# A two-layer GLA/gMLP trunk on Trainium2: in gMLP's first projection, three of five operands are made from turned ones instead of being turned

## The reference, cut to what matters

```python
for i in range(DEPTH):
    y = rms_norm(h, norm_mix[i])
    h = h + (gla_mixer if i == 0 else gmlp_mixer)(y, ...)
    h = h + swiglu(rms_norm(h, norm_ffn[i]), w_ffn_gate[i], w_ffn_up[i], w_ffn_down[i])

def gmlp_mixer(h, w_in, b_in, ln_g, ln_b, w_s, b_s, w_out):
    z = jax.nn.gelu(h @ w_in + b_in)          # w_in: 1024 x 6144
    u, v = z[..., :E], z[..., E:]             # E = 3072
    v = layer_norm(v, ln_g, ln_b)
    ...
    return (u * sv.reshape(B, S, E)) @ w_out
```

## Time and profile before

| | before |
|---|---|
| median of 3 runs | 2548.91 us (2548.80 to 2551.12) |
| the profiled execution | 2549.63 us, of which the span is 2547.8 us |
| TensorE (PE) busy | 2507.0 us, 98% of the span |
| VectorE (DVE), ScalarE (ACT), GpSimd (POOL) busy | 1742.6, 1097.1 and 1295.0 us |
| mean granted TensorE clock | 0.997 |

### The profile page before, as it was taken

One profiled execution on the slowest core, in us unless ns is written; L12 is line 12 of the kernel. 1 busy time (PEld: TensorE's weight loads), 2 busy tenths in 40 slices (PEclk: granted clock), 3 DMA queues, 4 the chain that ended last, 5 costly groups with the idle time before them and its releaser, 6 DMA issues.

```text
span 2547.8 us, 33431 instructions
## 1 busy us (share of the span) xinstructions
PE 2507.0 (98%) x11680; PEld 2079.3 (82%) x11680; DVE 1742.6 (68%) x2225; ACT 1097.1 (43%) x1943; POOL 1295.0 (51%) x984
## 2 busy tenths in 40 slices
PE   8999999999999999999999999999999999999998
PEld 6787888778888888888888888888888888888886
DVE  5255678877787765577665899865676877656556
ACT  4344555543333344454433333344544333334444
POOL 3234456645555554454666555544455555555543
PEclk9999999999999999999999999999999999999999
DMA  7674426336566558655987455687634666326864
GB/s 236 210 268 145 111 74 215 112 116 213 205 223 217 185 184 290 194 194 166 320 291 236 145 169 171 203 302 246 205 110 143 211 213 206 120 72 213 272 191 149
DMA packets 311259, 493.38 MB, mean 194 GB/s; under 512 B 32992, under 2 KB 132704, under 8 KB 311104
## 3 DMA queue, kind: packets, MB, share of 16 engines
q1 hardware_dynamic: 311104, 491.39, 58.0%
HBM read 328.24 MB, written 154.66 MB: 190 GB/s over the span
## 4 chain that ended last, share of the span: by engine, by line
PE 89%; DVE 4%; DMA 2%; issue 2%; ACT 1%; SPq 1%; POOL 0%; DVEq 0%; ACTq 0%
PE ps L657 28%; PE ps L659 28%; PE ps L658 28%; PE ps L2729 2%; DMA qk<-qk_scratch 2%; PE ps L2517 1%; PE ps L2588 1%; DVE r_all L1909 1%; DVE state L1848 0%; DVE zbuf L1821 0%; SPq L790 0%; DVE g_sb L1857 0%; DVE r_all L1884 0%; POOL w_lo_main L645 0%; DVE att L1810 0%
## 5 line engine op out<-in xcount | busy, mean ns | idle before, releaser
L733 POOL TENSOR_TENSOR ring_lo<-stg,ring_hi 128x512 fp32r<-128x512 f32 x666 | 953.7, 1434 | 897.1 <-ACT ring_hi L729 896.5
L729 ACT ACTIVATE ring_hi<-stg 128x512 fp32r<-128x512 f32 x666 | 420.6, 632 | 1060.1 <-PE ps L659 995.2
L657 PE MATMUL ps<-xh_all,ring_hi 128*128 128x512 f32 x1536 | 600.5, 391 | 1.2 <-DVE r_all L2283 0.9
L659 PE MATMUL ps<-xh_all,ring_lo 128*128 128x512 f32 x1536 | 597.8, 389 | 0.0
L658 PE MATMUL ps<-xl_all,ring_hi 128*128 128x512 f32 x1536 | 597.6, 389 | 0.0
L751 DVE TENSOR_TENSOR s_ring<-s_stage,s_ring 128x512 fp32r<-128x512 f32 x238 | 297.9, 1263 | 225.8 <-ACT s_ring L747 225.3
L657 PE MATMUL ps<-ring_hi,s_ring 128*128 128x512 f32 x1064 | 415.5, 391 | 3.1 <-DVE r_all L1909 1.6
L659 PE MATMUL ps<-ring_hi,s_ring 128*128 128x512 f32 x1064 | 414.1, 389 | 0.0
L658 PE MATMUL ps<-ring_lo,s_ring 128*128 128x512 f32 x1064 | 414.0, 389 | 0.0
L657 PEld LDWEIGHTS ps<-xh_all,ring_hi 128*128 128x128 f32 x1536 | 288.4, 188 | 61.0 <-POOL ring_lo L733 1.3
L659 PEld LDWEIGHTS ps<-xh_all,ring_lo 128*128 128x128 f32 x1536 | 288.3, 188 | 59.9
(11 more groups left out here) (262 smaller groups left out, 3642.6 us busy)
## 6 DMA issues: line engine op xcount, KB each, us to landing
s_stage<-h_scratch SPq DMA_DIRECT2D x238, 256.0 KB, 3.4
stg<-t_scratch SPq DMA_DIRECT2D x200, 256.0 KB, 3.4
h_scratch<-r_all SPq DMA_DIRECT2D x34, 1024.0 KB, 5.1
h_scratch<-r_all SPq DMA_DIRECT2D x80, 256.0 KB, 3.5
stg<-in_w_ffn_gate SPq DMA_DIRECT2D x34, 512.0 KB, 4.3
stg<-in_w_ffn_up SPq DMA_DIRECT2D x34, 512.0 KB, 5.7
stg<-in_w_ffn_down SPq DMA_DIRECT2D x66, 256.0 KB, 3.6
t_scratch<-r_all SPq DMA_DIRECT2D x28, 512.0 KB, 2.8
```

Of the source, the lines that this page charges most:

```text
L657: pe.matmul(bank, s_hi, m_hi, start=first, stop=False, skip_group_check=more)
L659: return pe.matmul(bank, s_lo, m_hi, start=False, stop=last, skip_group_check=more)
L729: nc.scalar.activation(weight_slot(ring_hi, g), weights(g), ACT.Copy).then_inc(wh_done, 1)
L733: nc.gpsimd.tensor_tensor(weight_slot(ring_lo, g), weights(g), f32(weight_slot(ring_hi, g)), ALU.subtract).then_inc(wl_done, 1)
```

## The change

- `V_TURNS` keeps eight turned tiles: S2 (r = 8 to 11) behind steps 3, 4 and 5, A22 (now r = 16 to 19) behind steps 9 and 10. S1, S4 and S3 are no longer turned.
- ScalarE now copies each turned A11, A12 and S2 tile twice, once as it is into a kept place (`v_kept`) and once into `xh`. VectorE makes the turned S1 = S2 + A11, S4 = A12 - S2 and S3 = A22 - S2 from those (`turned_sum1`, `turned_sum4`, `turned_sum3`), and `made_hi` and `made_lo` cut them, from SBUF instead of PSUM.
- `sum4` in `head` and GpSimd's `sum3` are gone for this phase. The statistics of the first quarter, `stat(k, 0, ...)`, move from j = 10 to j = 17 in all three blocks.
- Waits and counts follow: among them SP waits at i = 17 for 12 turned tiles instead of 16 and at i = 23 for all rests of x, and TensorE's first step of product 6 asks for 12 instead of 16 rests, product 5 for `sum3_done`, product 3 for 24 instead of 28.

```diff
+        a11_kept = place("a11_kept", XH_AT + 8 * TILE, [P, 4, BANK])
+
+        s2_kept = place("s2_kept", XH_AT + 24 * TILE, [P, 4, BANK])
...
-        TURNS = {"U": ("S2", "S4", "S1", "S3", "A22"), "V": ("S2", "S1", "S4", "S3", "A22")}
+        TURNS = {"U": ("S2", "S4", "S1", "S3", "A22"), "V": ("S2", "S1", "A22", "S4", "S3")}
...
-        V_TURNS = {3: (8, 9), 4: (10,), 5: (11, 12), 6: (13, 14, 15), 9: (16, 17), 10: (18, 19), 13: (20, 21, 22, 23),
-                   14: (24, 25, 26, 27)}
+
+        V_TURNS = {3: (8, 9), 4: (10,), 5: (11,), 9: (16, 17), 10: (18, 19)}
...
+        def turns_before(n):
+
+            return 28 * n - (12 if n >= 2 else 0)
+
+        def turn_count(n, kind, r):
+
+            return turns_before(n) + r + 1 - (4 if kind == "V" and r >= 16 else 0)
+
+        def sum1_count(n, k):
+            return 4 * n + (4 if n >= 2 else 0) + k
+
+        def v_kept(op, t):
+
+            return {"A11": a11_kept[:, t, :], "S1": a11_kept[:, t, :], "A12": r_all[:, 2 * t + 1, :],
+                    "S2": s2_kept[:, t, :], "S3": n_all[:, t, :], "S4": r_all[:, 8 + 2 * t, :]}[op]
...
-                    sp.wait_ge(op_turned, 28 + 8 + 8)
-                    sp.wait_ge(sum4_done, 8)
+                    sp.wait_ge(op_turned, turns_before(1) + 8 + 4)
+                if i == 23:
+                    sp.wait_ge(xl_done, 2 * 28)
...
-                if name in ("f0", "v", "f1"):
+                if name in ("f0", "f1"):
...
-                act.wait_ge(op_turned, 28 * n + r + 1)
+                act.wait_ge(op_turned, turn_count(n, kind, r))
                 if n == 0 and r == 0:
                     act.wait_ge(sl_done, 6 * AP)
+                if n == 1 and op != "A22":
+                    nc.scalar.activation(v_kept(op, t), ps[:, turn_bank(kind, r), :], ACT.Copy)
+                if n == 1 and op == "A22" and t == 0:
+                    act.wait_ge(xl_done, 28 + 16)
...
+            def made_hi(op, made):
+
+                for t in range(4):
+                    act.wait_ge(made, {"S1": 8 + t + 1, "S4": 4 + t + 1, "S3": 8}[op])
+                    nc.scalar.activation(xh(op)[:, :, tile(t)], k4(v_kept(op, t)), ACT.Copy).then_inc(xh_done, 1)
...
+                        if j == 7:
+                            made_hi("S1", sum1_done)
+                        if j == 12:
+                            made_hi("S4", sum4_done)
+                        if j == 14:
+                            made_hi("S3", sum3_done)
...
+            def made_lo(op):
+
+                r = 8 + 4 * TURNS["V"].index(op)
+                for t in range(4):
+                    dve.wait_ge(xh_done, 28 + r + t + 1)
+                    nc.vector.tensor_tensor(xl(op)[:, :, tile(t)], k4(v_kept(op, t)), f32(xh(op)[:, :, tile(t)]),
+                                            ALU.subtract).then_inc(xl_done, 1)
+
+            def turned_sum1(t):
+
+                dve.wait_ge(xh_done, 28 + 8 + t + 1)
+                nc.vector.tensor_tensor(v_kept("S1", t), v_kept("S2", t), v_kept("A11", t), ALU.add).then_inc(sum1_done, 1)
+
+            def turned_sum4(t):
+
+                nc.vector.tensor_tensor(v_kept("S4", t), v_kept("A12", t), v_kept("S2", t), ALU.subtract
+                                        ).then_inc(sum4_done, 1)
+
+            def turned_sum3(t):
+
+                dve.wait_ge(op_turned, turn_count(1, "V", 16 + t))
+                nc.vector.tensor_tensor(v_kept("S3", t), ps[:, turn_bank("V", 16 + t), :], v_kept("S2", t), ALU.subtract
+                                        ).then_inc(sum3_done, 1)
...
+                    if kind == "V":
+                        break
...
-                    if k == 0 and j < 8:
-                        for r in V_TURNS.get(j - 1, ()):
-                            if r > 10:
-                                turned_lo(n, "V", r)
+                    if k == 0 and j == 6:
+                        turned_lo(n, "V", 11)
+                        for t in range(4):
+                            turned_sum1(t)
...
-                        if k == 0:
-                            dve.wait_ge(sum3_done, 4 * n + 4)
...
-                    if j == 10:
-                        stat(k, 0, v_c11)
-                    if k == 0:
-                        for r in V_TURNS.get(j - 1, ()) if j in (10, 11) else ():
+                    if k == 0 and j == 9:
+                        made_lo("S1")
+                    if k == 0 and j in (10, 11):
+                        for r in V_TURNS[j - 1]:
                             turned_lo(n, "V", r)
+                            turned_sum3(r - 16)
+                    if k == 0 and j == 11:
+                        for t in range(4):
+                            turned_sum4(t)
                     if j == 12:
                         dve.wait_ge(mm_done, base + 28 * k + 12)
+                        if k == 0:
+                            dve.wait_ge(sum4_done, 4 * n + 4)
...
-                        for r in V_TURNS.get(j - 1, ()) if j in (14, 15) else ():
-                            turned_lo(n, "V", r)
+                    if k == 0 and j == 13:
+                        made_lo("S4")
+                    if k == 0 and j == 15:
+                        made_lo("S3")
...
                     if j == 16:
                         dve.wait_ge(mm_done, base + 28 * k + 16)
+                        if k == 0:
+                            dve.wait_ge(xl_done, 28 * (n + 1))
...
+                    if j == 17:
+                        stat(k, 0, v_c11)
...
-                        pe.wait_ge(xl_done, 28 * n + {1: 8, 2: 8, 6: 16, 5: 20, 3: 28, 7: 28, 4: 28}[q])
+                        pe.wait_ge(xl_done, 28 * n + {1: 8, 2: 8, 6: 12, 5: 20, 3: 24, 7: 28, 4: 28}[q])
...
+                                pe.wait_ge(sum3_done, 4 * n + 4)
...
-                            if r == 20:
-                                pe.wait_ge(v_added, 8)
```

More of the change, by code:

```diff
@@ L1021, in u_loads @@
                         if s == 0:
-                            sp.wait_ge(op_turned, 28 * (d - 1) + 8 + 4)
+                            sp.wait_ge(op_turned, turns_before(d - 1) + 8 + 4)
                             sp.wait_ge(sum4_done, 4 * d)
@@ L1027, in u_loads @@
                         if s == 0:
-                            sp.wait_ge(op_turned, 28 * (d - 1) + 8 + 12)
+                            sp.wait_ge(op_turned, turns_before(d - 1) + 8 + 12)
                         load_panels(name, s + 1, "bottom")
@@ L1035, in u_loads @@
                         if s == 1:
-                            sp.wait_ge(op_turned, 28 * d)
+                            sp.wait_ge(op_turned, turns_before(d - 1) + 28)
                         if unit(s, 0) is not None:
@@ L1580, in u_phase @@
                             if s == 1:
-                                act.wait_ge(op_turned, 28 * (n + 1))
+                                act.wait_ge(op_turned, turns_before(n) + 28)
                             snapshot(s, 3, 1, u_up("21", s), hs_done, act_count(name, s - 2, 3) if s >= 2 else 0)
@@ L1892, in turned_lo @@
                                         f32(xh(op)[:, :, tile(t)]), ALU.subtract).then_inc(xl_done, 1)
+            def made_lo(op):
[14 more added lines that the diff above has]
+                                        ).then_inc(sum3_done, 1)
             def sum2(n, kind, i):
-                dve.wait_ge(sum1_done, 4 * n + i + 1)
+                dve.wait_ge(sum1_done, sum1_count(n, i + 1))
                 nc.vector.tensor_tensor(turn_source(kind, 8 + i), n_all[:, i, :], r_all[:, 2 * i, :], ALU.subtract
@@ L1902, in sum4 @@
                 dve.wait_ge(sum2_done, 4 * n + i + 1)
-                dve.wait_ge(op_turned, 28 * n + 2 * i + 2)
+                dve.wait_ge(op_turned, turns_before(n) + 2 * i + 2)
                 nc.vector.tensor_tensor(r_all[:, 2 * i + 1, :], r_all[:, 2 * i + 1, :], turn_source(kind, 8 + i),
@@ L1981, in head @@
                             turned_lo(n, kind, r)
-                    if i == 1 and kind == "U":
+                    if kind == "V":
+                        break
+                    if i == 1:
                         turned_lo(n, kind, 11)
@@ L2583, in turn_op @@
                 else:
-                    pe.wait_ge({"S1": sum1_done, "S2": sum2_done, "S3": sum3_done, "S4": sum4_done}[op], 4 * n + t + 1)
+                    pe.wait_ge({"S1": sum1_done, "S2": sum2_done, "S3": sum3_done, "S4": sum4_done}[op],
+                               sum1_count(n, t + 1) if op == "S1" else 4 * n + t + 1)
                 wait(pe, xl_done, 28 * n + bank_before(kind, r))
```

## The result

The changed kernel takes 2556.69 us (median of 8 runs, 2555.89 to 2563.20) against 2549.99 us (8 runs, 2548.80 to 2552.00) for the kernel before on the same chip: a ratio of 1.0034, with a 95% interval of 1.0025 to 1.0043. It is slower by 6.7 us by the medians; the interval of the ratio is 6.4 to 11.0 us. The profiled execution took 2556.64 us, of which the span is 2554.9 us.

A forecast was written before the change was run, and what follows sets the result against it. TensorE, busy for 98% of the span, was taken to bound the kernel. A saving of 6.7 us and the added waits summed to +7.2 us on 2549.63, so 2556.8, a median of 2556.1; range 2546 to 2566.

The forecast's parts named there:

- turned tiles and the two old stalls: Phase v, TensorE: twelve fewer turned tiles (5.3 us) and both stalls (0.75 and 0.66 us) gone, together -6.7 us.
- step 12: Block 0 of phase v: TensorE waits for A22's rests and S3's sums, +0.3 us (0 to 1.5).
- step 16: Block 0 of phase v: TensorE waits for S4's rests from VectorE, +0.3 us (0 to 1.3).
- steps 22 to 24: Block 0: additions late because weight tiles and the unit's load stand behind SP's store, +6.2 us (3 to 8).
- step 32: Next block's first additions late on VectorE, delaying ScalarE's gelu and the copies this step needs, +1.5 us (0 to 2.5).
- step 52: Block 1: weight tile 50 late behind SP's store, so GpSimd's chain and an addition end late, +3.1 us (1 to 4.5).
- step 56: Block 1: VectorE's unit 7, `stat` and eight additions take 13.4 us against 10.9, +2.5 us (0 to 3).
- rival 3: TensorE's clock falls after long waits in phase v, adding 1 to 4.8 us, up to 2561; chance 0.15.
- Two inputs in SBUF: VectorE's rests of S1, S4, S3: 0.60 us each, plus one GpSimd instruction (1.25 us) per four.
- The case in which every rest meets a GpSimd instruction: Phase v: all twelve rests and eight sums shut out by GpSimd, making the sum +9.4 us.
- the lead holds: Rival: weight tiles loaded 19 us ahead arrive in time, only -6.1 us remains, 2542.8; chance 0.12.
- Half of it: Rival: block 0 loses 3 to 5 us, shorter loads and idle GpSimd save block 1, +0.6, 2549.5; chance 0.23.

The follow-up runs named there:

- e1: Changed kernel with SP's stores of the first quarter of v moved from behind weight tile 21 to behind tile 27: 2542.68 us.
- e2: Changed kernel with the first quarter's `stat` at j = 14 in block 0 and j = 10 in blocks 1 and 2: 2543.63 us.
- e3: Kernel before with one edit alone, the first quarter's `stat` at j = 17 in all blocks: 2556.90 us.
- e7: Changed kernel with VectorE's unit 1 behind the additions of j = 20 instead of ahead of them: 2557.03 us.
- e6: Changed kernel with the first quarter's `stat` at j = 14 in block 0, still at j = 17 in blocks 1 and 2: 2548.76 us.
- e5: Changed kernel with the first quarter's `stat` at j = 17 in block 0 alone, at j = 10 in blocks 1 and 2: 2550.41 us.

## Why the prediction was right, and where its terms were off

The cause and the total came out as forecast: 2556.69 us measured where 2556.1 was the forecast, +6.8 us on phase v where its terms had made +7.2. Not all of the terms did. Forecast and measured, us (measured waits from TensorE's timeline above; the saving from e1; the clock and the row above it worked out below):

| term | forecast | measured |
|---|---|---|
| turned tiles and the two old stalls | -6.7 | -6.8 |
| step 12 | +0.3 | +0.26 |
| step 16 | +0.3 | 0 |
| steps 22 to 24 | +6.2 | +5.53 |
| step 32 | +1.5 | 0 (1.7 in e2, 2.5 in e3) |
| step 52 | +3.1 | +0.98 |
| step 56 | +2.5 | +2.45 |
| what the recorded waits leave out | - | +0.7 |
| clock | 0 (rival 3) | +3.8 |
| sum | +7.2 | +6.9 |

**The saving** was right. e1 has the same list on TensorE and no late loads; its phase v runs from 1146.44 to 1379.23, 232.8 us, 6.6 less than 239.4. Take out the 0.26 us at step 12, and it is 6.8.

**Two inputs in SBUF.** By the rows a group of four was to take 4 x 0.60 and one GpSimd instruction, 3.65 us. VectorE's timeline of the kernel after has four such groups at 3.59 us and one, with GpSimd idle, at 2.48:

```profile
1184.07 3.59 DVE L1947 TENSOR_TENSOR r_all<-r_all,s_kept 128x512 f32<-128x512 f32 x4
...
1190.15 3.59 DVE L1937 TENSOR_TENSOR xl_all<-r_all,xh_all 128x512 fp32r<-128x512 f32 x4
...
1198.26 2.48 DVE L1937 TENSOR_TENSOR xl_all<-n_all,xh_all 128x512 fp32r<-128x512 f32 x4
```

Step 16 waits for S4's rests, the second line, which end at 1193.74, 1.5 us ahead of it. From S4's first sum (1184.07) to there the list took 9.7 us, what the forecast had with one GpSimd instruction per four; its +0.3 allowed for a GpSimd instruction in each step, 12.2, which did not come. The third line is S3's rests, which step 20 needs: GpSimd had no weight tile to cut then, since the loads were held up. In e1, where they weren't, the same four took 3.58 us. Where VectorE and GpSimd did meet, the bill was on GpSimd too: its instructions took 1.74 us instead of 1.29 from 1213.85 on, while VectorE made the unit. The Trainium skill, "SBUF — State Buffer" (section "Who interferes with whom"), says that the two shut each other out for a whole instruction; the trace agrees in kind, 3.59 against 2.48 us per four. The case in which every rest meets a GpSimd instruction, +9.4, didn't come, since GpSimd makes one rest per step at most.

**Block 0** by its stations, from the start of step 16 at 1195.2: `stat` done at 10.5 (forecast 11.9), tile 22 issued at 11.0 (12.4), GpSimd's chain done at 26.7 (26.4), the last addition at 27.4 (27.0), step 24 due at 22.0 and begun at 27.5. Two errors cancel: `stat` and with it SP's store came 1.4 us sooner, 1.1 of it because nothing contended with S3's rests (2.48 instead of 3.6), the rest from a shorter unit 0; and GpSimd took 11.8 us for eight instructions instead of 10.0, as the slower ones above show. These 1.8 us are the one to two that the unit was to add, and e7 shows them, but at another place than forecast: on GpSimd's chain, not behind the wait for the unit's load.

**Step 32** is the term that failed outright. The prediction counted from step 24's delayed start at full speed: 1222.73 + 21.8 = 1244.5. ScalarE's copies, for which step 32 waits, begin only at 1245.10:

```profile
1245.10 2.49 ACT L1649 ACTIVATE z_all<-ps 128x512 f32<-128x512 f32 x4
```

In e2 step 32 begins 0.7 us behind the start of these copies (1240.46 against 1239.75). By that, an estimate, TensorE at full clock would have stood for about 1.3 us, close to the 1.5 forecast. The lower clock behind step 24 cost it 2.2 us on the way (below), so it came at 1246.7 and found the copies done. The clock and this wait are not added, the longer of the two counts. In e2 and e3, where TensorE had not been held up at step 24, the wait is there, 1.7 and 2.5 us.

**Step 52** was oversized, 3.1 for 0.98. The step that failed is the length of unit 6: it was given the time of the earlier trace rows (the additions begin at 1278.41, unit 6's last subtraction ends at 1285.5), which put `stat` 7.3 us behind the start of step 44. It began there 5.1 us behind it, and what comes after it, the rest of tile 50 included, came 2.2 us sooner than forecast; GpSimd's chain took 10.05 us, as forecast. Unit 6 met an idle GpSimd and took 2.5 us (1282.04 to 1284.56); that contention too the stand of SP took away. SP's first pause came as forecast (1181 to 1206, measured 1180.5 to 1204.0); the second, forecast from 1265 to 1287, lasted from 1271.8 to 1285.3, 13.5 us instead of 22. **Step 56** was right: from there the list on VectorE has a fixed length.

**The clock** was a rival with a chance of 0.15, and it is what happened, together with the forecast and not in place of it. Between step 12 and the end of v the changed kernel has 8.96 us of waits (5.53 + 0.98 + 2.45); its phase is 246.22 - 232.79 = 13.4 us longer than e1's. No instruction differs, so 4.5 us are left beside the recorded waits. A part of these 4.5 is waiting as well. In e1 the 72 steps from step 12 on (1183.18 to 1379.23) take 196.05 us, 2.723 each. A recorded wait begins at the modelled end of the matmul before, and from step 52 to step 56, at a granted clock of 1.00, four steps took 13.57 us where e1's take 10.89, 2.68 more for a recorded 2.45. That is 0.23 for each wait, 0.7 for three. The other 3.8 us are the matmuls that ran at 1.2 instead of 2.4 GHz: 2.2 us behind step 24 (its 28 steps to step 52 took 79.61 us, 1.2 of them at step 52's wait, where e1's take 76.24) and 1.6 behind step 56 (77.86 for the last 28 steps). The price for each was put at 2.4 us, and the second fall was looked for at step 52, where the clock stayed. The forecast had a row for it, a fall after 3.40 us, and a stall of 6.2 us in its own sum; with the two side by side the fall should have been part of the forecast. That the total came out is luck: steps 16, 24, 32 and 52 were given 4.6 us too much, about what the clock and the unrecorded part of the waits took, 4.5.

**The other rivals.** That the lead holds (0.12) is false: the lead of 19 us in the queue is less than the 23.5 us that SP stood, and step 24 waited. Half of it (0.23) was right about an idle GpSimd in block 1, but the loads were hardly shorter (3.2 us from the issue of tiles 22 and 50 to ScalarE's copy of them, where it needed 2.5), and block 1 was not saved: its waits of 0.98 and 2.45 us and the low clock behind them are in the changed kernel, and a late `stat` in blocks 1 and 2 costs 5.7 us by e6.

What remains open is step 32: that the slower matmuls behind step 24 covered it is worked out from the timelines, and no kernel was run that has step 24's wait at full clock.

## What to carry to other kernels

Before an instruction is moved, look at whose queue waits for its signal, not only at who reads its data. Here no computation read the statistics before the end of phase v, but a store waited for them in a queue that issues in order, and weight loads stood behind that store: 2.4 us of work on VectorE, whose place made no more than half a us at step 12, cost 13 to 14 us where they were put. The cure was cheap, one number in SP's list (tile 21 to tile 27), and with it the change is worth 6.5 us: e1 beats both kernels.

When a wait of two us or more is in a forecast for TensorE, count what its clock does afterwards as a term of its own, but set it against the later waits that it covers, and remember that a delay upstream also empties the engines downstream, which are then faster than in the profile of before.

## What was not expected of the hardware

In phase v of these runs the granted clock fell with waits of 2.16 (e3, e7), 2.45 and 5.53 (changed kernel), 2.52 (e3), 3.74 (e7) and 5.54 us (e5), and stayed at 1.00 with waits of 0.71, 0.98, 1.0, 1.06 and 1.7 us. The price does not follow the length of the wait: in the changed kernel 5.53 us of waiting brought 2.2 us of slower matmuls behind it, and 2.45 us brought 1.6. Behind the long wait a part of the low clock fell into the wait itself, where it costs nothing; behind the short one (0.79 for eight us) all of it met matmuls.

One VectorE instruction with two inputs in SBUF can stand behind several of GpSimd's. In e2 and e3 the first subtraction of unit 2 took 4.91 us, while GpSimd made four rests in one stretch of 5.0 us; in the changed kernel, where GpSimd had rests to make too, it took 1.16. All four subtractions together took 6.8 us in e2 and 6.3 in the changed kernel.

After SP's stand the DMA engines moved 404 GB/s at a share of 1.06 (1226 to 1230 us in the kernel after). That is no new speed: the kernel before reaches 407 GB/s in some windows of four us (1316 to 1320), and the 300 GB/s and 0.86 of the earlier trace rows are the mean of 76 us. From 1204 to 1244 us the kernel after moved 333 GB/s where the kernel before moved 275, so a transfer that is put off in this phase is made up faster than the prediction assumed.
